# Adding sparse attention's mask to the biases by GpSimd's accumulating transfers for twelve of sixteen heads

## What is computed

```python
score = jnp.where(causal[None], score, -jnp.inf)
_, idx = lax.top_k(score, topk)
c_sel = jax.vmap(lambda cb, ib: cb[ib])(c, idx)
...
bias = jnp.moveaxis(rel_bias[t5_bucket(dist)], -1, 2)
logits = jnp.einsum('bqhc,bqkc->bqhk', q_lat_b, c_sel).astype(jnp.float32) \
    + bias.astype(jnp.float32)
logits = jnp.where((dist >= 0)[:, :, None, :], logits, -jnp.inf)
p = jax.nn.softmax(logits, axis=-1).astype(c.dtype)
return jnp.einsum('bqhk,bqkc->bqhc', p, c_sel)
```

## Time and profile before

| | |
|---|---|
| three executions | 864.71, 865.09, 865.21 us |
| the profiled execution | 865.02 us, of which the span is 863.2 us |
| PE busy | 857.0 us, 99% of the span |
| DVE, ACT, POOL busy | 635.0, 465.8, 73.6 us |
| the chain that ended last | PE 97%, DVE 1%, POOL 1% |
| the mask's matmuls (L723) | 16, from 322.0 to 352.6 us |
| the stage of the heads | about 322 to 366 us |

### The profile page before, as it was taken

How to read it: one execution, slowest core, us unless ns; L and a number is a source line. 1 busy time by engine, 2 the same in 40 slices (tenths; PEclk the granted TensorE clock), 3 DMA queues, 4 the chain that set the end, 5 groups by cost and what they waited for, 6 DMA issues and landing times.

```text
span 863.2 us, 12973 instructions
## 1 busy us (share of the span) xinstructions
PE 857.0 (99%) x5036; PEld 736.2 (85%) x5036; DVE 635.0 (74%) x1028; ACT 465.8 (54%) x746; POOL 73.6 (9%) x71
## 2 busy tenths in 40 slices
PE   8999999999999999999999999999999999999998
PEld 7998888888887987788888888888898888888887
DVE  5969799888865496478759775564477897898874
ACT  6796564444444569546546544354467673544540
POOL 3010100000000045310001000032200000000000
PEclk9999999999999999999999999999999999999999
DMA  8635678776642455456749555420425355454531
GB/s 342 235 117 192 252 267 314 281 262 233 212 174 96 150 183 163 174 207 246 262 150 322 185 214 189 171 98 25 178 109 182 132 194 196 158 200 182 197 143 49
DMA packets 32181, 164.81 MB, mean 191 GB/s; under 512 B 3572, under 2 KB 9976, under 8 KB 15352
## 3 DMA queue, kind: packets, MB, share of 16 engines
q1 hardware_dynamic: 32112, 163.97, 53.0%
q10 hardware_dynamic: 8, 0.00, 0.0%
HBM read 162.92 MB, written 1.05 MB: 190 GB/s over the span
## 4 chain that ended last, share of the span: by engine, by line
PE 97%; DVE 1%; POOL 1%; ACT 0%; DMA 0%; issue 0%; DVEq 0%
PE ps L346 16%; PE ps L348 16%; PE ps L347 16%; PE ps L333 12%; PE ps L315 7%; PE ps L317 6%; PE ps L316 6%; PE ps L335 6%; PE ps L484 2%; PE ps L904 1%; PE ps L929 1%; PE ps L913 1%; PE ps L387 1%; PE ps L750 1%; PE ps L727 1%; PE ps L735 1%
## 5 line engine op out<-in xcount | busy, mean ns | idle before, releaser
L1716 DVE TENSOR_TENSOR WL<-RAW,WH 128x1024 fp32r<-128x1024 f32 x258 | 304.5, 1216 | 52.3 <-ACT WH L1117 52.1
L1117 ACT CAST WH<-RAW 128x1024 fp32r<-128x1024 f32 (+1 forms) x264 | 262.4, 1043 | 71.0 <-PE ps L348 54.9
L333 PE MATMUL ps<-XA,WH 128*128 128x512 f32 x448 | 140.6, 395 | 0.0
L315 PE MATMUL ps<-XA,WH 128*128 128x256 f32 x464 | 134.2, 289 | 0.1
L317 PE MATMUL ps<-XA,WL 128*128 128x256 f32 x464 | 131.3, 283 | 0.0
L316 PE MATMUL ps<-XA,WH 128*128 128x256 f32 x464 | 131.2, 283 | 0.0
L335 PEld LDWEIGHTS ps<-XA,WL 128*128 128x128 f32 x448 | 84.1, 188 | 19.6
L346 PE MATMUL ps<-WH,HTh 128*128 128x512 f32 x256 | 100.2, 391 | 0.0
L347 PE MATMUL ps<-WL,HTh 128*128 128x512 f32 x256 | 99.7, 389 | 0.0
L348 PE MATMUL ps<-WH,HTl 128*128 128x512 f32 x256 | 99.7, 389 | 0.0
L315 PEld LDWEIGHTS ps<-XA,WH 128*128 128x128 f32 x464 | 88.9, 192 | 7.4 <-issue 6.5
(11 more groups left out here) (283 smaller groups left out, 1319.8 us busy)
## 6 DMA issues: line engine op xcount, KB each, us to landing
RAW<-in_w_dram SPq DMA_DIRECT2D x129, 1024.0 KB, 4.9
AD<-in_w_dram SPq DMA_DIRECT2D x8, 512.0 KB, 7.3
CX<-in_w_dram SPq DMA_DIRECT2D x6, 512.0 KB, 4.8
TB<-in_w_dram SPq DMA_DIRECT2D x5, 512.0 KB, 4.8
AW<-in_w_dram SPq DMA_DIRECT2D x5, 512.0 KB, 5.7
RI<-in_w_dram SPq DMA_DIRECT2D x2, 1024.0 KB, 11.2
GB<-in_gb_dram SPq DMA_DIRECT2D x4, 512.0 KB, 6.4
BI<-in_dbias_dram SPq DMA_DIRECT2D x16, 128.0 KB, 4.0
```

The source lines that it names most:

```text
L315: T.e.matmul(dst, h, xh[:, k, :], start=k == 0, stop=False)
L333: T.e.matmul(M.PS[bank + m][:, :], parts[i][0], M.X2[:, k + i, :], start=k + i == 0, stop=False)
L1117: A.e.copy(M.WH[:, c.s, sl], M.RAW[:, c.r, sl]).then_inc(*S.hi.tick(key, a))
L1716: D.e.tensor_tensor(M.WL[:, c.s, sl], M.RAW[:, c.r, sl], M.WH[:, c.s, sl].bitcast(F32), ALU.subtract).then_inc(*S.lo.tick(key, a))
```

## The change

Three edits belong together.

The mask's matmuls stay for the first two pairs (heads 0 to 3) and go for the other six. For heads 4 to 15, GpSimd issues one transfer per head from `MS` to the head's bias in SBUF that adds as it writes (`masked(h)`). DVE then waits for that transfer (`S.masked`) where it waited for the bias.

The biases get six places, each a tile of its own, so that head h uses place h % 6. The two new ones lie behind the other tiles of this stage.

SP's list is changed: six heads' biases instead of four behind the second quarter of the query weights, heads 6 to 11 ahead of chunk ("wo", 2) and behind ("wo", 1), heads 12 to 15 ahead of ("wo", 3) and behind ("wo", 2). A bias waits for DVE's reading of head h - 6.

A few counting semaphores are shared between stages, which adds no instruction.

```diff
@@ tensor_dsa, logits(m)
-        for t in range(2):
-            T.wait_ge(*S.mask.at(t))
-        T.wait_ge(*S.idr.at())
-        for h2 in range(2):
-            T.e.matmul(M.PS[4 + h2][:, 0:384], M.IDR[:, :], M.MS[:, :], start=True, stop=False)
+        early = 2 * m < MASKED
+        if early:
+            for t in range(2):
+                T.wait_ge(*S.mask.at(t))
+            T.wait_ge(*S.idr.at())
+            for h2 in range(2):
+                T.e.matmul(M.PS[4 + h2][:, 0:384], M.IDR[:, :], M.MS[:, :], start=True, stop=False)
@@ DVE, logits(h)
-        D.wait_ge(S.bi[h % 4], 32 * (h // 4 + 1))
+        if h < MASKED:
+            D.wait_ge(S.bi[h % 6], 32 * (h // 6 + 1))
+        else:
+            D.wait_ge(*masked_at(S, h))
@@ pool_program
+MASKED = 4
+def masked_at(S, h):
+    return S.masked[h % 2], 16 * ((h - MASKED) // 2 + 1)
...
+    def masked(h):
+        for t in range(2):
+            P.wait_ge(*S.mask.at(t))
+        P.wait_ge(S.bi[h % 6], 32 * (h // 6 + 1))
+        if h >= MASKED + 2:
+            P.wait_ge(*masked_at(S, h - 2))
+        P.e.dma_start(M.BIS[h % 6][:, :], M.MS[:, :].bitcast(F32), accum_op=ALU.add).then_inc(S.masked[h % 2], 16)
...
+    masked(4)
+    masked(5)
     for h in range(16):
         normalised(h)
+        if h % 2 and h < 11:
+            masked(h + 5)
+            masked(h + 6)
@@ sync_program
-        if h >= 4:
-            Y.wait_ge(*S.ttr.at(h - 4, 1))
+        if h >= 6:
+            Y.wait_ge(*S.ttr.at(h - 6, 1))
...
-            for h in range(4):
+            for h in range(6):
                 bias(h)
     gain(3)
-    for key, heads in ((("wo", 0), ()), (("wo", 1), ()), (("wo", 2), (4, 5, 6, 7)), (("wo", 3), (8, 9, 10, 11)), (("up", 1, 0), (12, 13, 14, 15)),
-                       (("up", 1, 1), ())):
+    for key, heads in ((("wo", 0), ()), (("wo", 1), range(6, 12)), (("wo", 2), range(12, 16)), (("wo", 3), ()), (("up", 1, 0), ()), (("up", 1, 1), ())):
```

More of the change, by code:

```diff
@@ L199, in __init__ @@
         self.MS = self.tile("MS", [128, 384], F32R)
-        self.BI = self.tile("BI", [128, 4, 384])
+        self.BIS = [self.tile(f"BI{i}", [128, 384]) for i in range(4)]
         at = self.top
@@ L208, in __init__ @@
         self.RLh = self.tile("RLh", [128, 2, 384])
+        behind = self.top
         self.top = at
@@ L212, in __init__ @@
         self.PT = self.tile("PT", [128, 4, 384])
+        self.top = max(self.top, behind)
+        self.BIS += [self.tile(f"BI{i}", [128, 384]) for i in range(4, 6)]
         self.top = arena
@@ L726, in logits @@
                 hp = 64 * h2
-                made = T.e.matmul(M.PS[4 + h2][:, a0:a1], M.QT[hp:hp + 64, m, q0:q0 + 128], M.KD[hp:hp + 64, m, 0:a1 - a0], start=False, stop=q0 > 0)
+                made = T.e.matmul(M.PS[4 + h2][:, a0:a1], M.QT[hp:hp + 64, m, q0:q0 + 128], M.KD[hp:hp + 64, m, 0:a1 - a0],
+                                  start=not early, stop=not early or q0 > 0)
         made.then_inc(*S.lg.tick(m))
@@ L2141, in logits @@
         for t, (a0, a1) in enumerate(SPANS):
-            D.e.tensor_tensor_reduce(M.LG[:, h % 4, a0:a1], M.PS[4 + h % 2][:, a0:a1], M.BI[:, h % 4, a0:a1], -1.0, 3e38,
+            D.e.tensor_tensor_reduce(M.LG[:, h % 4, a0:a1], M.PS[4 + h % 2][:, a0:a1], M.BIS[h % 6][:, a0:a1], -1.0, 3e38,
                                      ALU.add, ALU.min, M.stat("nm", h, t)).then_inc(*S.ttr.tick(h, t))
@@ L2690, in bias @@
             Y.wait_ge(*S.ada.at("rows", 0))
-        if h >= 4:
-            Y.wait_ge(*S.ttr.at(h - 4, 1))
-        Y.e.dma_start(M.BI[:, h % 4, 0:128], D["dbias"][h, :, 128:256]).then_inc(S.bi[h % 4], 16)
-        Y.e.dma_start(M.BI[:, h % 4, 128:384], D["dbias"][h]).then_inc(S.bi[h % 4], 16)
+        if h >= 6:
+            Y.wait_ge(*S.ttr.at(h - 6, 1))
+        Y.e.dma_start(M.BIS[h % 6][:, 0:128], D["dbias"][h, :, 128:256]).then_inc(S.bi[h % 6], 16)
+        Y.e.dma_start(M.BIS[h % 6][:, 128:384], D["dbias"][h]).then_inc(S.bi[h % 6], 16)
     def context(t):
@@ L2821, in signals @@
     S.raw = [landed(f"raw{r}") for r in range(NRAW)]
-    S.g, S.bi = [landed(f"g{i}") for i in range(2)], [landed(f"bi{i}") for i in range(4)]
+    S.g, S.bi = [landed(f"g{i}") for i in range(2)], [landed(f"bi{i}") for i in range(6)]
+    S.masked = [landed(f"masked{i}") for i in range(2)]
     S.aw = [landed(f"aw{i}") for i in range(3)]
@@ L2921, in signals @@
     S.pads = then(S.qgain, one)
-    S.nttr, S.nrec = count("nttr", both), count("nrec", both)
-    S.yat, S.yal = count("yat", blocks), count("yal", blocks)
-    S.glu, S.cvp, S.ys, S.ysl, S.sbm = (count(n, range(2)) for n in ("glu", "cvp", "ys", "ysl", "sbm"))
+    S.nttr, S.nrec = then(S.ttr, both), then(S.rec, both)
+    S.yat, S.yal = then(S.y, blocks), then(S.ybl, blocks)
+    S.glu, S.cvp, S.ys, S.sbm = (count(n, range(2)) for n in ("glu", "cvp", "ys", "sbm"))
+    S.ysl = then(S.otl, range(2))
     S.tap = count("tap", [(ch, k) for j in range(2) for k in range(1, 31) for ch in (2 * j, 2 * j + 1)])
```

## The result

The changed kernel takes 874.85 us (median of five, 873.15 to 875.17) against 864.71 us in the same round: a ratio of 1.0113, interval 1.0102 to 1.0124. It is slower by 10.1 us, where 1.25 us less was forecast and 868.0 us was the end of the range. The profiled execution has a span of 873.1 us, 9.9 us over that of before. All of the 9.9 us arises in the stage of the heads: one and the same instruction of ACT behind it starts at 370.01 us before and at 379.87 us now, and from there to the end both kernels take 493.2 us.

What follows compares the result with a forecast made beforehand. PE was taken as the bound, with GpSimd the feeder to watch. 1.74 us less for matmuls, plus 0.1 and 0.4 us of lateness, gave -1.25 us: 865.02 to 863.8 us, range 863.0 to 868.0 us.

Steps and rivals of the forecast that it cites:

- The matmuls: On PE, six pairs of mask matmuls go, 2.09 us; the first pair's 0.35 us is lost at turn(2), leaving 1.74.
- GpSimd's hold: Each of twelve mask transfers holds GpSimd for its issue, taken as 1.05 us, making PE 0.1 and 0.4 us late.
- d: How long issuing one accumulating mask transfer holds GpSimd; taken as 1.05 us, with nothing late below 0.9 us.
- the walk: Head-by-head timing of GpSimd's masks and multiplications against PE's turns: 0.1 us late at head 6, together 0.4 at head 8.
- the far end: An issue holding GpSimd 2.2 us, until landing: some +7 us, 872 us, left out of the range.
- What is hidden: Mask landings, SP's four more issues and the moved weight chunks were each said to cost nothing.
- The walk's first item: Masks 6 and 7 start at 327.44 us, their biases landed in 2.2 to 2.8 us, and end before head 2's turn.
- SP's order: Four more bias issues (1.9 us) and later weight chunks cost nothing; ("wo", 2) there at 338.8 us, within ACT's idle time.
- Rival 1: Dearer issues make GpSimd the bound, PE waiting at turn(4), turn(6), turn(8): 866.4 or 868 us; chance 0.28.
- Rival 2: DVE's two-tile operations hold GpSimd's issues, lengthening two or three mask windows by up to 1 us: 866.3 us; chance 0.08.
- Rivals 3 and 4: Full 2.09 us gain, turn(2) included, 862.9 us, chance 0.04; 64-row matmuls 0.3 us dearer behind transposes, 865.0 us, chance 0.03.
- The marks named: Signs of error: PE waiting over 1 us for GpSimd, dearer eight matmuls, or ACT waiting for ("wo", 2) and PE for ACT.

Runs made afterwards that it cites:

- e2: Changed kernel without the twelve mask transfers and without any mask for heads 4 to 15: 863.23 us.
- e14: Changed kernel with three weight loads cut to 256 of 2048 columns and a counter for each of six places, no wait for an earlier mask: 863.66 us.
- e13: Changed kernel with chunks ("wo", 2), ("wo", 3) and ("up", 1, 0) cut to 256 of 2048 columns: 864.08 us.
- e7: Changed kernel with GpSimd adding the mask itself by a 128x384 tensor_tensor in the same places, no mask transfers: 865.46 us.
- e3: Changed kernel with a counter for each of the six places, so GpSimd waits for no earlier mask: 868.70 us.
- e4: Changed kernel with the mask transfers as plain copies that overwrite the bias, no addition: 868.42 us.
- e10: Changed kernel with the mask left with PE for heads 4 and 5 too, so ten mask transfers: 872.84 us.
- e11: Changed kernel with 20 more matmuls of 384 columns on PE, results unused, ahead of turn(6) and of turn(10): 872.58 us.
- e1: Changed kernel with six bias places and SP's new order only; PE masks all heads, no mask transfers: 864.64 us.
- e6: Changed kernel with a counter for each place, no wait for an earlier mask, and chunk ("wo", 2) ahead of the biases of heads 6 to 15: 867.49 us.
- e17: Changed kernel with three loads split in four, GpSimd waiting for the mask four heads before, chunk ("wo", 2) ahead of biases 6 to 15: 869.85 us.

## Why the prediction was wrong

**The matmuls: right.** Six pairs at 0.35 us, one of them lost at `turn(2)`, and the 64-row matmuls no dearer. The forecast of 1.74 us for that part measured 1.42 (e2), which is the same within the noise.

**GpSimd's hold: near in size, a little too high.** d was taken as 1.05 us; the issue took 0.87 at the median and 1.19 at most. The Trainium skill's figure that the prediction named beside it, about 1 us for the emission (DMA: Bandwidth & Descriptors, section on latency), was near as well. With small loads the kernel came to 863.66 (e14) and 864.08 us (e13). How much is lost at a given d is less sure. For d = 1.05 us the walk lets PE wait 1.0 us in all, and with e7's additions of 1.01 us it waited 2.5. And the slope that the sum states, 0.6 us for each 0.1 us, makes +5.7 and not +7 at d = 2.2, so the far end would be 870.7 and not 872 us.

**"What is hidden": the step that failed.** It said of the masks: "A mask must have landed before DVE's logits of its head. For masks 9 and 11 there are some 5 us from issue to need, more than the 4.8 us of the slowest bias; a late one would hold DVE, and PE asks for DVE's result only a step later. Nothing." Two things were wrong in it, and a third in the walk ahead of it.
- The one who waits. The order printed ahead of the prediction says `waits d_masked0` on GpSimd's transfers. Mask h + 2 may not be issued until mask h has landed, and behind it in GpSimd's list stand the multiplications that PE wants next. The working asked what DVE needs of a landing and never what GpSimd does. Without this wait 6.2 us of the 10 are gone (874.85 to 868.70, e3).
- The size. The landing was bounded by 4.8 us, the slowest of the bias loads. Those come from another memory, by another queue and without an addition. A mask took 3.0 us undisturbed and 7.4 to 9.9 beside a chunk of 1 MB. The rows had a sign of it: the biases with up to 4.8 us were issued right behind chunk ("wo", 3), at 334.36 us, and those of 324 to 331 us, with only the end of a chunk on its way, took 2.8 at most. So 4.8 us was a disturbed landing of a cheaper transfer, and no bound. The same paragraph moved chunks ("wo", 2) and ("wo", 3) right onto the masks' time and looked only at when the chunk would be there, not at what it would meet. With three chunks cut all is gone (874.85 to 864.08, e13), so this is the root, and the wait is how most of it reaches PE. The parts don't add up to 10 us, since each edit (e3, e4, e13) takes away a link of the same chain.
- The biases. The walk's first item has those of heads 6 and 7 landed in 2.2 to 2.8 us, "nothing is queued ahead of them". Masks 4 and 5 were on their way, the biases took up to 4.8 us, and PE waited 1.14 us at `turn(2)`. With these two masks' work left with PE the kernel is 2.0 us faster (e10).

**The clock: not in the prediction.** It priced each wait at its length. Two waits of 3.5 us cost some 2 us more, since PE worked at 1.2 GHz behind each (e11).

**SP's order: right that it costs nothing by itself** (e1), wrong that it therefore counts for nothing. Chunk ("wo", 2) was to be there at 338.8 us and landed at 340.61, and ACT waited 1.12 us for it; PE did not wait for ACT.

**The rivals.** Rival 1 had the right victim, PE at `turn(6)`, with the wrong cause: it tied the loss to the length of the issue, and its highest figure, 872 us, belonged to an engine held until the data has landed. Something near that did happen, through a counter instead of the instruction. I had left this end out of the range. Rival 2, the hold by DVE's two-input operations, did not show: the issues took 0.87 us at the median. Rivals 3 and 4 are out by e2.

**The marks named.** "I am wrong if PE waits for GpSimd by more than 1 us in all": it waited 8.8 us.

## What to carry to other kernels

A transfer that an engine both issues and waits for, to keep one counter per transfer in flight, puts the landing into that engine's own list; ask what is queued behind that wait, and not only who reads the data. A small transfer's landing, read where the queues are empty, is no bound where a load of 1 MB is on its way: put the two on one time axis before the sum is made, above all when the same change moves the loads. And a wait on PE can cost more than its length: behind each of the two of 3.5 us here the work ran at half the clock.

## What the runs showed of the hardware that was not expected

**Small transfers beside large ones.** 192 KB added within SBUF land in 3.0 us alone and in 7.4 to 9.9 us beside 1 MB loads, which themselves take 7.0 to 9.5 us and not 4.9. Both are slowed; the transfer engines' share was 0.99 in 345 to 355 us at 259 and 298 GB/s.

**A transfer that adds.** It isn't a copy at the same price. The same 2.36 MB took 1.7% of the transfer engines' time in 1728 packets with the addition, and 0.7% in 768 without it (e4).

**DVE beside GpSimd.** DVE's low part of the weights, 1.2 us in the earlier trace rows, took 3.03 and 4.06 us where GpSimd's multiplications ran back to back behind a late mask:

```profile
343.67 3.03 DVE L1722 TENSOR_TENSOR WL<-RAW,WH 128x1024 fp32r<-128x1024 f32 x1
...
358.31 4.06 DVE L1722 TENSOR_TENSOR WL<-RAW,WH 128x1024 fp32r<-128x1024 f32 x1
```

The prediction had used the rule of the Trainium skill (SBUF — State Buffer, section "Who interferes with whom") that such an operation contends with GpSimd's reads, for the harm to GpSimd; here the harm to DVE was the larger, a factor of 2.5 to 3.4. Who began first differs. In the earlier trace rows DVE's operation began at 329.63 us, ahead of GpSimd's at 329.80, and kept its 1.20 us while GpSimd's took 1.30. In the two cases here GpSimd's multiplications had begun, at 343.39 and 358.15 us. That this decides it is not shown by three cases.

**An issue that is held.** In e6 GpSimd's issues of masks 8 to 11 took 2.5 to 3.5 us each, overlapping in pairs, 7.0 us for the four. DVE stood idle for 3.3 us of these. GpSimd's timeline, two issues each:

```profile
333.75 3.39 POOL L2648 DMA_DIRECT2D BI<-MS  x2
...
336.75 4.04 POOL L2648 DMA_DIRECT2D BI<-MS  x2
```

Two or three earlier masks were on their way each time. But in e14 and e17 issues behind as many took 0.85 to 1.66 us, so that number alone doesn't explain it. DVE's low parts of the weights, which read two tiles, ran from 333.01 to 334.97 and from 339.69 to 340.90 us, so they cover the start of the one pair and the end of the other, and not the rest. The cause stays open.
